# The last projection of a two-block fp32 layer as one level of Strassen's product: seven quarter products in place of eight

## The reference

```python
p_a = jnp.einsum('bsw,wd->bsd', out_a, w_branch_sb[layer])
p_b = jnp.einsum('bsw,wd->bsd', out_b, w_branch_ret[layer])
merged = (jax.nn.sigmoid(m_sb + b_merge[layer, 0]) * p_a
          + jax.nn.sigmoid(m_ret + b_merge[layer, 1]) * p_b)
x = x + jnp.einsum('bsd,de->bse', merged, w_out[layer])
```

## Time and profile before

| | before |
|---|---|
| three runs, us | 2207.37, 2200.14, 2201.62; median 2201.62 |
| profiled execution: own time, us | 2203.64 |
| its span (first to last instruction), us | 2201.8 |
| busy: PE, DVE, ACT, POOL | 97%, 50%, 43%, 16% |
| mean granted TensorE clock | 0.983 of full |
| HBM traffic | 148.31 MB read, 51.68 MB written |

### The profile page before, as it was taken

How to read it: one execution, slowest core, us unless ns; L and a number is a source line. 1 busy time by engine, 2 the same in 40 slices (tenths; PEclk the granted TensorE clock), 3 DMA queues, 4 the chain that set the end, 5 groups by cost and what they waited for, 6 DMA issues and landing times.

```text
span 2201.8 us, 29272 instructions
## 1 busy us (share of the span) xinstructions
PE 2137.4 (97%) x11719; PEld 1773.8 (81%) x11719; DVE 1110.8 (50%) x2061; ACT 938.8 (43%) x1708; POOL 349.5 (16%) x526
## 2 busy tenths in 40 slices
PE   7999989998988999999999999999999999999999
PEld 5789878876987888878888787888888878888887
DVE  5776465642465445665466645546415252434441
ACT  4665454544462425654465544642232323232220
POOL 5010361452021100000000000005103030110011
PEclk9999999998798999999999999999999999999999
DMA  4455444346613321111112211120311112343222
GB/s 141 132 177 191 128 145 133 93 108 243 233 39 110 112 72 36 37 53 58 48 39 67 63 48 39 39 71 16 116 48 53 43 50 80 113 156 133 92 92 86
DMA packets 159240, 205.57 MB, mean 93 GB/s; under 512 B 35104, under 2 KB 113408, under 8 KB 157568
## 3 DMA queue, kind: packets, MB, share of 16 engines
q1 hardware_dynamic: 139888, 136.51, 19.8%
q0 software_dynamic: 19216, 67.19, 9.3%
HBM read 148.31 MB, written 51.68 MB: 91 GB/s over the span
## 4 chain that ended last, share of the span: by engine, by line
PE 91%; DVE 4%; ACT 2%; issue 1%; DMA 1%; POOL 1%; SPq 0%; DVEq 0%; POOLq 0%; ACTq 0%
PE PS L1866 13%; PE PS L1868 13%; PE PS L1867 13%; PE PS L1859 10%; PE PS L1861 10%; PE PS L1860 10%; PE PS L1824 5%; PE PS L2148 3%; PE PS L2127 3%; PE PS L1957 1%; PE PS L2180 1%; PE PS L2193 1%; DVE WH L2583 1%; PE PS L1932 1%; PE PS L2167 1%
## 5 line engine op out<-in xcount | busy, mean ns | idle before, releaser
L1866 PE MATMUL PS<-WH,HH 128*128 128x512 f32 (+1 forms) x1344 | 532.2, 396 | 2.4 <-DVE HL L2606 1.7
L1868 PE MATMUL PS<-WH,HL 128*128 128x512 f32 (+1 forms) x1344 | 512.6, 381 | 0.0
L1867 PE MATMUL PS<-WH,HH 128*128 128x512 f32 (+1 forms) x1344 | 511.5, 381 | 0.0
L1859 PE MATMUL PS<-HH,WH 128*128 128x512 f32 (+1 forms) x1040 | 426.1, 410 | 17.7 <-DVE WH L2583 12.1
L1861 PE MATMUL PS<-HH,WH 128*128 128x512 f32 (+1 forms) x1040 | 408.3, 393 | 0.0
L1860 PE MATMUL PS<-HL,WH 128*128 128x512 f32 (+1 forms) x1040 | 407.8, 392 | 0.0
L1866 PEld LDWEIGHTS PS<-WH,HH 128*128 128x128 f32 x1344 | 253.8, 189 | 55.6 <-issue 13.2
L1868 PEld LDWEIGHTS PS<-WH,HL 128*128 128x128 f32 x1344 | 253.3, 188 | 44.6
L1867 PEld LDWEIGHTS PS<-WH,HH 128*128 128x128 f32 x1344 | 254.2, 189 | 36.9
L2583 DVE SCALAR_TENSOR_TENSOR WH<-RAW,WK,WH 128x512 fp32r<-128x512 f32 (+2 forms) x248 | 184.2, 772 | 197.1 <-ACT WH L2202 196.5
L1859 PEld LDWEIGHTS PS<-HH,WH 128*128 128x128 f32 (+1 forms) x1040 | 195.5, 188 | 60.0 <-DVE WH L2583 13.3
(11 more groups left out here) (321 smaller groups left out, 2781.6 us busy)
## 6 DMA issues: line engine op xcount, KB each, us to landing
RAW<-in_w_in SPq DMA_DIRECT2D x200, 256.0 KB, 3.2
RAW<-in_w_out SPq DMA_DIRECT2D x32, 256.0 KB, 3.5
sig_d<-WK POOLq DMA_DIRECT2D x32, 256.0 KB, 2.3
WK<-sig_d POOLq DMA_DIRECT2D x32, 256.0 KB, 3.3
WK<-in_rpb POOLq DMA_DIRECT2D x16, 480.0 KB, 4.5
RAW<-in_w_in SPq DMA_DIRECT2D x32, 192.0 KB, 4.8
dnc_d<-TM SPq DMA_DIRECT2D x12, 512.0 KB, 4.3
TM<-dnc_d SPq DMA_DIRECT2D x10, 512.0 KB, 4.2
```

What stands on the lines that cost most here:

```text
L1859: e.matmul(ps, wh, hh, start=k == 0, stop=False)
L1866: e.matmul(ps, hh, wt[:, 0:width], start=k == 0, stop=False)
L1867: e.matmul(ps, hh, wt[:, 512:512 + width], start=False, stop=False)
L1868: mm = e.matmul(ps, hl, wt[:, 0:width], start=False, stop=k == 7)
```

## The change

`o0` and `o1` become one block `o` (number 35) computed by one level of Strassen's product in Winograd's form. `merged` is cut into quarters A11, A12, A21, A22 (512 tokens x 512 channels: the first digit is the half of tokens, the second the half of channels), `w_out` into B11 to B22, the output into C11 to C22. Seven products of 512 x 512 x 512 replace eight; each is four tiles (t) of four slabs (c) of three matmuls:

- j = 0: A11 B11; 1: A12 B21; 2: S2 T2; 3: S3 T3; 4: S1 T1; 5: S4 B22; 6: A22 T4
- S1 = A21 + A22, S2 = S1 - A11 (VectorE, 128x2048, item `ys`); S4 = A12 - S2, then S3 = A22 - S2 (GpSimd, 128x2048, items `ys 4`, `ys 3`)
- T1, T2 (`yt 0`, `yt 1`), T3 (`yt 2`), T4 (`yt 3`): four GpSimd operations of 128x512 each
- `ya j`: split of the left operand of product j into hi and lo, 128x2048 on ScalarE and VectorE
- `yx`, `yu`: sums of the products, U3 and U2, from PSUM into SBUF (ScalarE, VectorE); `yr n`: GpSimd adds U to the loaded tile of `x1`
- `ed O n`: output tile n (0 to 15) = bank + `sgt`, VectorE; `yo`: one 2 MB load of the right half of `w_out` by SyncE, in place of eight of 256 KB

The diff, cut to what the prediction speaks of ("..." marks what is left out):

```diff
+LEFT = ((0, 0), (4, 0), (0, 512), (4, 512), (0, 0), (4, 0), (0, 512))
...
-        for th in range(2):
-            for k in range(8):
-                yield has("ed", BLOCK["rt1"], (3, th))
-                put("mc", th, k)
-                yield
+        for k in range(8):
+            yield has("ed", BLOCK["rt1"], (3, 0))
+            put("mc", 0, k)
+            yield
...
+    def sums_ahead(t):
+        i = tiles_of(O_BLOCK - 1).index(t)
+        if 1 <= i < 5:
+            put("yt", 0, i - 1)
+            put("yt", 1, i - 1)
+
+    def right(j):
+        for c in range(4):
+            put("w", W_O + 4 * j + c)
+
+    def output():
...
+        for n in range(4):
+            put("fd", O_BLOCK, n)
+        put("ys", 1)
+        put("ys", 2)
+        for t in range(4):
+            put("yp", 0, t)
+            put("yx", t)
+            put("yr", t)
+        put("ya", 2)
+        right(2)
+        put("ys", 4)
+        for c in range(4):
+            put("yt", 2, c)
+        put("ys", 3)
+        for t in range(4):
+            put("yp", 1, t)
+            put("ed", O_BLOCK, t)
+            put("fd", O_BLOCK, 4 + t)
+        put("ya", 3)
+        right(3)
+        for c in range(4):
+            put("yt", 3, c)
+        for t in range(4):
+            put("yp", 2, t)
+            put("yu", 2, t)
+        put("ya", 4)
+        right(4)
+        for t in range(4):
+            put("yp", 3, t)
+            put("yu", 3, t)
+            put("yr", 4 + t)
+        put("ya", 5)
+        right(5)
+        for t in range(4):
+            put("yp", 4, t)
+            put("ed", O_BLOCK, 4 + t)
+            put("yu", 4, t)
+            put("fd", O_BLOCK, 8 + t)
+            put("yr", 8 + t)
+        put("ya", 6)
+        right(6)
+        for t in range(4):
+            put("yp", 5, t)
+            put("ed", O_BLOCK, 8 + t)
+            put("fd", O_BLOCK, 12 + t)
+            put("yr", 12 + t)
+        for t in range(4):
+            put("yp", 6, t)
+            put("ed", O_BLOCK, 12 + t)
...
+                elif kind == "yo":
+                    w.wait_ge(*at["st", "ob", 7, 1, "t"])
...
+                elif kind == "yp":
...
+                    if j < 2:
+                        released(w, before)
+                    elif j == 2:
+                        w.wait_ge(*at["yx", t, "x"])
+                    elif j == 3:
+                        w.wait_ge(*at["ed", O_BLOCK, t, "out"])
+                    else:
+                        w.wait_ge(*at["yu", j - 2, t, "u"])
...
+                    for c in range(4):
+                        n = W_O + 4 * j + c
+                        w.wait_ge(*at["w", n, "lo"])
...
+                elif kind == "ys" and a[0] > 2:
+                    w.wait_ge(*at["ys", 2, "s"])
+                    if a[0] == 4:
+                        w.wait_ge(*at["mc", 0, 7, "lo"])
+                        e.tensor_tensor(A12, A12, A11, ALU.subtract).then_inc(*w.sig(*item, "s"))
+                    else:
+                        w.wait_ge(*at["ys", 4, "s"])
+                        w.wait_ge(*at["ya", 2, "lo"])
+                        e.tensor_tensor(A11, A22, A11, ALU.subtract).then_inc(*w.sig(*item, "s"))
...
+                elif kind == "yr":
+                    n = a[0]
+                    i, nth = fed(O_BLOCK, n)
+                    w.wait_ge(c_st[i], 16 * (nth + 1))
...
+                    e.tensor_tensor(sgt[i], sgt[i], u, ALU.add).then_inc(*w.sig(*item, "r"))
...
-                    g, cb = (b - 31) * 8 + nth - 4, (b - 31) % 2
+                    g = (b - 31) * 8 + nth - 4
                     if g >= 0:
-                        before = 31 + g // 8
-                        w.wait_ge(*at["ed", before, tiles_of(before)[g % 8], "out"])
+                        before = min(31 + g // 8, O_BLOCK)
+                        w.wait_ge(*at["ed", before, tiles_of(before)[g - (before - 31) * 8], "out"])
```

More of the change, by code:

```diff
@@ L176, in tiles_of @@
         return [(c, th) for th in range(2) for c in range(4)]
+    if BLOCKS[b] == "o":
+        return list(range(16))
     return list(range(8)) + ([(3, 0), (3, 1)] if BLOCKS[b][:2] == "na" else [])
@@ L207, with quarter @@
 }
+GROUPS["out"] = ("yp", "yx", "yu", "yr", "ys", "yt", "ya")
+O_BLOCK = BLOCK["o"]
+W_O = 8 * O_BLOCK
+LEFT = ((0, 0), (4, 0), (0, 512), (4, 512), (0, 0), (4, 0), (0, 512))
+RIGHT = ("b11", "b21", "t2", "t3", "t1", "b22", "t4")
+QUARTERS = ((0, 0), (1, 1), (0, 1), (1, 0))
+def quarter(n):
+    th, cb = QUARTERS[n // 4]
+    return th * 4 + n % 4, cb
 GROUP = {kind: g for g, kinds in GROUPS.items() for kind in kinds}
@@ L303, in signals @@
         "rm": [("dve", "o")],
+        "yp": [("pe", "done")],
+        "yx": [("act", "x")],
+        "yu": [("dve", "u")],
+        "yr": [("pool", "r")],
+        "ys": [("dve" if a and a[0] in (1, 2) else "pool", "s")],
+        "yt": [("pool", "t")],
+        "ya": [("act", "hi"), ("dve", "lo")],
     }.get(kind, [])
@@ L1190, in schedule @@
         if b == 34:
+            put("yo")
             plan.spawn(merge_in())
-        gemm(b, feeds(b), left.append if b == 32 else None)
+        gemm(b, feeds(b), left.append if b == 32 else sums_ahead if b == 34 else None)
+    plan.drain()
+    output()
     put("end")
@@ L1397, in build, with by_columns, quad, right_raw @@
         ot = [area.take(512) for _ in range(4)]
+        T2, U3, U2 = (area.take(2048) for _ in range(3))
+        assert area.at <= WKW - 512
+        B12, B22 = TM[:, 0, 0:2048], TM[:, 0, 2048:4096]
+        def by_columns(a):
+            return a.rearrange("p (k t) -> p k t", k=4)
+        def quad(kh, th):
+            return TM[:, 1 + kh, :].rearrange("p (k t) -> p k t", k=4)[:, :, th * 512:(th + 1) * 512]
+        A11, A12, A21, A22 = quad(0, 0), quad(1, 0), quad(0, 1), quad(1, 1)
+        S_OUT = {1: A21, 2: A11, 3: A11, 4: A12}
+        LEFT_RAW = {2: A11, 3: A11, 4: A21, 5: A12, 6: A22}
+        def right_raw(j, c):
+            part = slice(c * 512, (c + 1) * 512)
+            return (RAW[:, c, :], RAW[:, 4 + c, :], T2[:, part], RAW[:, c, :], B12[:, part], B22[:, part],
+                    RAW[:, 4 + c, :])[j]
         gam = [1.0 - 2.0 ** (-5.0 - h) for h in range(4)]
@@ L1681, in _ @@
                         x_load(n + NRAW)
-                    if not 72 <= n + NRAW < 76:
+                    if not 72 <= n + NRAW < 76 and n < W_O:
                         load(n + NRAW)
@@ L2606, in _ @@
                     tt(HLb[:, k, :], mixed[k], HHb[:, k, :].bitcast(F32), ALU.subtract).then_inc(*w.sig(*item, "lo"))
+                elif kind == "ys" and a[0] < 3:
+                    if a[0] == 1:
+                        w.wait_ge(*at["ed", BLOCK["rt1"], (3, 1), "out"])
+                        tt(A21, A21, A22, ALU.add).then_inc(*w.sig(*item, "s"))
+                    else:
+                        w.wait_ge(*at["ys", 1, "s"])
+                        w.wait_ge(*at["mc", 0, 3, "lo"])
+                        tt(A11, A21, A11, ALU.subtract).then_inc(*w.sig(*item, "s"))
+                elif kind == "ya":
+                    j = a[0]
+                    k0, col0 = LEFT[j]
+                    w.wait_ge(*at[(*item, "hi")])
+                    hi, lo = (x[:, k0:k0 + 4, col0:col0 + 512] for x in (HHb, HLb))
+                    tt(lo, LEFT_RAW[j], hi.bitcast(F32), ALU.subtract).then_inc(*w.sig(*item, "lo"))
+                elif kind == "yu":
+                    j, t = a
+                    part = slice(t * 512, (t + 1) * 512)
+                    w.wait_ge(*at["yp", j, t, "done"])
+                    if j == 2:
+                        w.wait_ge(*at["yx", t, "x"])
+                    elif j == 3:
+                        w.wait_ge(*at["yu", 2, t, "u"])
+                        w.wait_ge(*at["yr", t, "r"])
+                    else:
+                        w.wait_ge(*at["yu", 2, t, "u"])
+                    given_u, made = {2: (U3, U2), 3: (U2, U3), 4: (U2, U2)}[j]
+                    tt(made[:, part], given_u[:, part], bank(place["yp", j, t][0]),
+                       ALU.add).then_inc(*w.sig(*item, "u"))
                 elif kind == "mc":
@@ L2661, in _ @@
                     b, t = a
+                    name = BLOCKS[b]
+                    if name == "o":
+                        j = (1, 4, 5, 6)[t // 4]
+                        i, _ = fed(b, t)
+                        w.wait_ge(*at["yp", j, t % 4, "done"])
+                        w.wait_ge(*at["yr", t, "r"])
+                        w.wait_ge(c_ot[t % 4], 16 * (t // 4))
+                        tt(ot[t % 4], bank(place["yp", j, t % 4][0]), sgt[i], ALU.add).then_inc(*w.sig(*item, "out"))
+                        continue
                     ps = bank(place["tile", b, t][0])
-                    name = BLOCKS[b]
                     w.wait_ge(*at["g", b, t, 7, "done"])
```

118 lines of the change are left out of this document (101 added, 17 removed).

## The result

| | before | changed |
|---|---|---|
| median of the runs, us | 2201.96 (2200.14 to 2207.37, 4 runs) | 2219.65 (2215.92 to 2222.96, 4 runs) |
| ratio, 95% interval | | 1.0072 [1.0053, 1.0091] |
| profiled execution: own time, span, us | 2203.64, 2201.8 | 2218.77, 2216.8 |
| first matmul of the last projection, T0 | 2109.3 | 2108.0 |
| its last matmul starts, after T0 | 86.8 | 84.5 |

Slower by 0.72%, 15.8 us of 2202 by the ratio and 16.2 us by the length of the stage; 16.1 was forecast. The two medians are 17.7 us apart, and 2219.65 is 2 us over the forecast's 2217.7. Ahead of T0 the kernels do nearly the same, but T0 moves by itself: in the profiled executions of this study it lies between 2106.9 and 2115.5 us.

What follows compares the result with a forecast made beforehand. TensorE was taken to bound the kernel, busy 97% of the span. Removing 48 matmuls saves 10.9 us, but stalls and GpSimd's landing waits put the last issue at 104.3 against 88.2, 16.1 slower: 2217.7 us, range 2205 to 2224.

Steps and rivals of the forecast that it cites:

- landing of the 2 MB load: SyncE's single load, behind all its other loads: priced between 3.5 and 28 us, taken as 10.
- seven turns: GpSimd, yr 9 to yr 15: each output, load, landing and addition takes 5.1 us, 35.7 in all.
- The chain: End of the last projection: GpSimd waits for each landing on the spot, 5.1 us a tile against TensorE's 2.7.
- The port: Shared SBUF port: VectorE operations with two SBUF inputs and GpSimd's take turns, so their times add up.
- The first rival: Turns at the port do not bite, products 2 and 3 come in time: 4.2 us slower, 2205.8; chance 0.16.
- The two stalls: TensorE waits for VectorE's splits before products 2 and 3: 3.3 us, then 5.5; product 3 ends 8.8 behind.
- The clock: TensorE's clock falls in its stalls, losing 3.6 us that passes to the end: 19.7 slower, 2221.3; chance 0.14.
- The tail: Behind the last output's issue, 4.3 us to the span's end, taken as unchanged.
- The arithmetic: The sum's last issue at 104.3, 16.1 us slower; landings all of 4.0 would give 23 slower.
- The landing: x1 tile loads: 3.3 us from the rows kept; the skill's estimate of 2.6 would give 10.5 slower.
- The faster rival: TensorE sets the end, needing GpSimd turns under 3.6 us: 10.9 us less, 2190.7; chance 0.04.
- At nothing: Work added beside other work, such as eight GpSimd yt of 1.2 us in block 34, costs no time.

Runs made afterwards that it cites:

- e1: Changed kernel with yr 8 to 11 written behind their four loads and yr 12 to 15 behind theirs; stage 92.3 us, ratio to before 1.0002.
- e5: Changed kernel with yr 8 to 15 adding only 8 of 512 columns, landing waits kept; stage 99.4 us in its second execution.
- e7: e1 with S4 and S3 on VectorE, plus five GpSimd memsets of 128x2048 where GpSimd had S4; stage 85.3 us, one execution.
- e3: e1 with S4 and S3 on VectorE and the split of S2 and three T2 slabs ahead of product 0; ratio to before 0.9975.
- e10: e9 with GpSimd's four T4 additions also held back until the four slabs of T3 are split; stage 82.1 us, ratio to before 0.9945.
- e9: e8 with late splits again and GpSimd's T3 additions held until the T2 slabs are split; stage 83.6 us, ratio to before 0.9940.
- e8: e3 with the x1 tiles of outputs 12 to 15 loaded into T2 right behind yt 3; stage 83.3 us, ratio to before 0.9961.

## Why the prediction was right

Its sum beside the rows, term by term, in us after T0; the landing of the 2 MB load, the seven turns and the last row are durations:

| term | forecast | changed kernel |
|---|---|---|
| landing of the 2 MB load | 10 | 10.2 |
| `ya 2` ends | 19.8 | 19.8 |
| the four slabs of T2 are split | 27.0 | 25.8 |
| `ys 3` ends | 31.5 | 30.3 |
| the four slabs of T3 are split | 43.4 | 41.1 |
| product 3's last result used (`yu 3`) | 53.2 | 52.9 |
| `yr 8` ends | 66.8 | 64.5 |
| seven turns | 35.7 | 37.5 |
| the last output is issued | 104.3 | 103.6 |
| from there to the end of the span | 4.3 | 5.2 |

- **The chain** was right in place, cause and size. e1 takes it away and 16.5 us go; e5 shows the landing as its largest term. Six of seven turns were 4.9 to 5.2 us, one 6.9, with a landing of 5.05 that no row of before had; why that one was late stays open.
- **The port** was right in cause, less so in form. The first rival (4.2 slower, the operations do not collide) falls with the changed kernel's own trace (`ya 2` 6.32 us), and e7 shows that it is GpSimd's reading. What I had too high is the price of a pair that takes turns: 1.2 + 0.6 = 1.8 us forecast, 6.08 / 4 = 1.5 measured. Half of this is GpSimd's addition for T3 or T4, 1.05 us in a run (4.22 / 4); the other half is that the two overlap in part. And the splits of T3 took no turns at all, as said above. The two stalls before products 2 and 3 were 2.2 and 4.6 us, with 3.3 and 5.5 forecast.
- **Between `yu 3` and `yr 8`** lie the other 2 us by which `yr 8` came sooner. I had `yr 6` and `yr 7` fall between `ya 5` and its four splits, 7.6 us in all. Only `yr 7` did, and the stretch took 5.8.
- **The clock** rival was right in kind and small in size. After the stretch in which TensorE was busy for 0.99 of 4 us its granted clock fell to 0.79 and 0.78, and seven matmuls stood 0.43 us apart in place of 0.23 (1.2 in place of 2.4 GHz): 7 x 0.2 = 1.4 us, not 3.6. That is most of why product 3 ended only 0.3 us sooner than forecast though its slabs came 2.3 us sooner; so TensorE's whole loss, 8.5 us where 8.8 was forecast, is close by cancellation.
- **The tail** I took as unchanged. It is 0.9 us longer where four outputs leave together (changed kernel and e3 both 5.2), which I had not counted. That and the longer turns (0.9 and 1.8 us more) cancel against the 2.3 us by which `yr 8` came sooner, so that 16.2 against 16.1 is partly luck: the terms were off by 1 to 2 us each.
- **The arithmetic.** By its own terms the last output is issued at 102.5 + 3 x 0.54 = 104.1, 15.9 slower; and landings of 4.0 us would give 16.1 + 8 x 0.7 = 21.7, not 23. Neither moves the range by as much as 2 us.
- **The landing.** The eight x1 loads of the turns landed 3.3 us after the start of their issue in the median, 2.8 after its end. The estimate of 2.6 us that the prediction works out from the Trainium skill (DMA: Bandwidth & Descriptors, Anatomy of one DMA, not the opening table), and the 10.5 us slower in all that went with it, do not agree with the trace.
- **The faster rival** needed a turn under 3.6 us. The shortest measured was 4.9, and with the addition cut to 8 columns still 3.9 to 4.4. It came true only where the landing waits were written elsewhere.
- **At nothing** was right for block 34: TensorE shows no gap there, with GpSimd busy for 13.6 of the 20 us from 2070, which hold its eight additions.

## What to carry to other kernels

Where each engine walks one list in order, a wait belongs to an engine as much as an operation does. Moving the wait for a load from VectorE, which was idle for two thirds of that stage, to GpSimd, which also sends the next load, turned a hidden landing of 3.3 us into eight that add up. When matrix work is traded for additions, cost these by the engine's order and the port it shares, not by the engine's idle share: GpSimd was idle for 82% of this kernel and still ended it. Keep GpSimd's SBUF reads away from those VectorE operations with two SBUF inputs that TensorE waits for; a semaphore wait that makes GpSimd later made the stage 1.5 us shorter here (e10 against e9).

## What was new about the hardware

- Reads collide, writes don't: a 128x2048 subtraction on VectorE took 2.29 us beside GpSimd memsets and 6.32 us beside a GpSimd subtraction of 4.61 us.
- A pair of 512-wide operations that took turns, 1.05 us on GpSimd and 0.6 on VectorE in runs of their own, took 1.5 us, a little less than the sum. But turns are not assured: a VectorE split that started 0.08 us ahead of four GpSimd additions took 4.86 us, until all four were through.
- Four 256 KB outputs issued back to back end the span 5.2 us after the last issue, one alone 4.3 to 4.7 (before, e8, e9, e10).
- One 2 MB load issued by SyncE landed after 9.6 to 10.7 us in all eleven changed kernels, against 3.5 for 256 KB. It stood right behind five 256 KB loads, issued in the 3 us before it, so this is not the time of such a load alone.
